# Gate sort as single-pass matmuls on 64 stacked rows, and layer 2's squares folded to one tile on VectorE

## Chip, cores, metric

One NeuronCore of a Trainium2 chip. The metric is the device time in microseconds of one execution; lower is better. TensorE is called PE in the profile, its weight loads PEld, VectorE DVE, ScalarE ACT, GpSimd POOL, and SyncE, which issues the DMAs, SP.

## What is computed

Two layers of a bidirectional hybrid encoder on 256 positions of 2048 channels in float32, and a final RMS norm. Cut to what matters here:

```
def rms_norm(x, w):
    y = xf * lax.rsqrt(jnp.mean(xf * xf, axis=-1, keepdims=True) + EPS)
    return (y * w.astype(jnp.float32)).astype(x.dtype)

def hybrid_layer(x, norm_w, w_in, b_in, ...):
    hn = rms_norm(x, norm_w)
    u = jnp.einsum("bsd,dn->bsn", hn, w_in) + b_in
    q, k, v, o, z_a, gates, glu_a, glu_b, z_b, g_a, g_b = jnp.split(u, _OFFSETS, axis=-1)
    ...
    gates = gates.astype(f32).reshape(B, S, 4, H).transpose(2, 0, 3, 1)
    i_fw, f_fw, i_bw, f_bw = gates[0], gates[1], gates[2], gates[3]
    flip = lambda t: jnp.flip(t, axis=2)
    both = lambda fw, bw: jnp.concatenate([fw, flip(bw)], axis=0)
    h2 = mlstm_chunkwise(both(qh, qh), both(kh, kh), both(vh, vh),
                         both(i_fw, i_bw), jax.nn.log_sigmoid(both(f_fw, f_bw)))
    ...
    merged = jax.nn.sigmoid(g_a) * y_a + jax.nn.sigmoid(g_b) * y_b
    return x + jnp.einsum("bsd,de->bse", merged, w_out)
```

`y_a` comes out of `h2`, `y_b` out of a gated depthwise convolution. There are 4 heads, so `gates` are 16 channels: input and forget gate, forward and backward, for each head. The backward ones are used with the positions reversed.

## The kernel before

**Data and pairs.** Activations lie with channels on the 128 partitions and the 256 positions along the free axis. Almost all of the work is products with weights of 2048 rows. The weights come in pairs of tiles (2048 rows by 256 columns), 104 pairs per layer, numbered n; each pair comes in four quarters c, which SP loads into RAW (line 324) as soon as the low part of the previous pair's quarter has been made. A float32 product is made of float32r products of high and low parts: ScalarE casts RAW to the high part (split_hi, line 438), VectorE subtracts to get the low part (split_lo, line 841), and TensorE multiplies the high part with the high and low activations at once (512 columns, line 1576) and the low part with the high activations (256 columns, line 1579). The inner step of `multiply` is two of the first kind and two of the second, 16 such instructions in a quarter. After a pair, ScalarE copies the low sums (low_half, lines 447 and 451) and VectorE adds the two (pair_out, line 848, or scaled_out, line 962, in the first pairs).

**Order.** Each engine runs its own list, written out by hand; semaphores order them. Between the splits of each pair the lists of ScalarE and VectorE hold the other work of that stage, and an engine never skips a waiting instruction. TensorE waits for `lo_made` at each quarter.

**Gates.** After the second pair of a layer TensorE multiplies the 16 gate columns, high and low part (line 1720, 128 rows by 32 columns), into one PSUM bank. ScalarE copies one half (line 568). VectorE's make_gates adds the halves (line 1016), multiplies by the norm's scale (line 1018) and adds the bias (line 1021), which sets `gates_made`. GATES are 32 rows of float32, the high columns' sums on the first 16 and the low ones' on the others. TensorE's sort_gates (lines 1731 and 1732) puts the gates in rows by head and direction, with the positions reversed for the backward half, by multiplying with the 0/1 matrix PICK: four float32 matmuls, with 32 rows and 8 columns of weights and 256 moving columns each. PICK adds rows 0 to 15 and 16 to 31 up by the way. In layer 1 sort_gates comes before the first quarter of pair 3, and turn_params (transposes of parameters, line 1640), before the third quarter of pair 2, waits for `gates_made` as well, since it writes the same PSUM. In layer 2 sort_gates comes before the last quarter of pair 2. ScalarE reads the sorted rows (lines 624, 625), makes the forget gates' logarithm (lines 627, 629), and VectorE the running sums and maxima (lines 1097 to 1116); ScalarE's Exp (line 635) closes this part. In this stretch VectorE's list also has the normalised activations (line 949) and their low parts (line 954), and ScalarE's the high parts (norm_high, line 552).

**The norm of layer 2.** While the last projection of layer 1 gives X two tiles at a time (lines 1509, 1512), ScalarE squares them (square_duo, line 468, into two of the four tiles of EW) and VectorE adds them to the two tiles of ACC (add_squares, line 940), except for the last pair of tiles. `sq_added` counts these additions. TensorE's sum_squares, before the third quarter of layer 2's first pair, sums over the channels: four float32 matmuls with a matrix of ones (line 1647), for ACC's two tiles and for EW's two with the last squares. ScalarE takes the root (line 485), VectorE the reciprocal (line 1068), and norm_group follows. Behind the squares ScalarE weighs X (line 474) and casts it (line 481) and loads the table for the root (line 822); VectorE makes the low parts (weighed_low, line 871).

**The last norm** has its own path at the end of layer 2 (lines 1526, 1533, 1655).

What sets PE's order around the sort in layer 1 and 2, and the sum:

```
if l == 0:
    multiply(n0, 2, YC, before=turn_params)
    multiply(n0, 3, Hs, h_lo, 0, late=sort_gates, at=0)
else:
    multiply(n0, 2, Hs, h_lo, l * 4, late=sort_gates)
```

Of the kernel before, what the change touches and what calls it, by code (L numbers as in the profile page):

```python
# [30 lines left out]
F32 = mybir.dt.float32  # L31
F32R = mybir.dt.float32r
ALU = mybir.AluOpType
# [4 lines left out]
L = 2  # L38
# [4 lines left out]
H = 4  # L43
HT = KT // H
# [7 lines left out]
NG = 4 * H  # L52
# [12 lines left out]
N_GLU, N_HEAD, N_GA, N_ZB, N_GB, N_OUT = KT, 10 * H, KT, KT // 2, KT, KT // 2  # L65
# [49 lines left out]
def build_trunk(nc, x, norm_w, w_in, b_in, qk_conv_w, mlstm_norm_w, w_a, dw_w, dw_b,  # L115
                ln_w, ln_b, w_b, w_out, final_norm_w, out):
    with ExitStack() as ctx:
        def sb(name, shape, dt=F32):
            return ctx.enter_context(nc.sbuf_tensor(name, shape, dt))
# [14 lines left out]
        MX = nc.alloc_sbuf_tensor_at("MX", [P, KT, S], F32R, offset=m_at)  # L134
        HEAD = sb("HEAD", [P, KT, S])
        QB = sb("QB", [P, HT, S])
        EW = sb("EW", [P, HT, S])
# [3 lines left out]
        ACC = sb("ACC", [P, 2, S])  # L141
# [4 lines left out]
        ONES = sb("ONES", [P, P])  # L146
        GBIAS = sb("GBIAS", [2 * NG, L])
        SEL = sb("SEL", [2 * NG, NG])
        PICK = sb("PICK", [2 * NG, 4, 2 * H])
        TCOL = sb("TCOL", [P, ST, 2 * H])  # L150
        ECOL = sb("ECOL", [P, 2, H, ST])
        R4 = sb("R4", [P, 2 * ST])[:]
# [17 lines left out]
        GW = M[:, 2 * HT, :].rearrange("p (k g) -> p k g", k=KT)  # L170

        GLOW, GATES = M[0:2 * NG, 2 * HT + 1, :], M[0:2 * NG, 2 * HT + 2, :]
        F_R, A_R, I_R, G_R, Z_R, N_R = (M[0:2 * H, i, :] for i in range(6))
        STACK = M[:, 2 * HT + 3, :]
        C_R = CROW[:]
# [29 lines left out]
        squared = sem("squared")  # L205
        sq_added = sem("sq_added")
        summed = sem("summed")
# [8 lines left out]
        gates_made, grows_mm = sem("gates_made"), sem("grows_mm")  # L216
# [216 lines left out]
        def _(act):  # L433
# [29 lines left out]

            def square_duo(l, d):

                act.wait_ge(sq_added, l * (N_OUT - 1) + (d + 1))
                q = d % 2
                nc.scalar.activation(EW[:, 2 * q:2 * q + 2, :], X[:, 2 * d:2 * d + 2, :], ACT.Square
                                     ).then_inc(squared, 1)
# [76 lines left out]
            for l in range(L):  # L546
# [254 lines left out]
                for d in range(N_OUT):  # L801
                    n = l * NP + AT_OUT
                    if d < N_OUT - 1 or l < L - 1:
                        split_rest(n, d, 0)
                    else:
                        nc.scalar.activation(R4[:, 2:3], EPSC[:], ACT.Sqrt)
                        act.wait_ge(sq_added, l * (N_OUT - 1) + (d + 1))
                        for t in range(2):
                            act.wait_ge(tile_out, t + 1)
                            nc.scalar.activation(EW[:, 2 + t, :], X[:, 2 * d + t, :], ACT.Square  # L810
                                                 ).then_inc(squared, 1)
                            nc.scalar.activation(HEAD[:, 2 * d + t, :], X[:, 2 * d + t, :], ACT.Identity,
                                                 scale=PAR[:, L * PARS + 2 * d + t:L * PARS + 2 * d + t + 1]
                                                 ).then_inc(xw_made, 1)
                        continue
                    act.wait_ge(pairs_out, n + (d + 3))
                    square_duo(l, d)
                    weigh_duo(l, d, (l + 1) * PARS + NORM_W + 2 * d)
                    if l < L - 1:
                        weighed_high(l + 1, d, xw_made, l * N_OUT + (d + 1))  # L820
# [13 lines left out]
        def _(dve):  # L834
            steps = Steps(dve, dve_steps)
            v = nc.vector
# [22 lines left out]
            dve.sem_inc(m_sum, 1)  # L859
            dve.wait_ge(ident_made, 1)  # L860
            steps.mark(v.tensor_tensor(SEL[:], IDENT[0:2 * NG, 0:NG], IDENT[0:2 * NG, NG:2 * NG], ALU.add))
            steps.mark(v.memset(PICK[:], 0.0))
            dve.wait_ge(nw_turned, 1)
            steps.mark(v.tensor_copy(NW[:], px[:, 3, 0:KT]))
            steps.wait()
# [2 lines left out]
            def weighed_low(at, d):  # L868

                dve.wait_ge(xw_hi, at * N_OUT + (d + 1))  # L870
                v.tensor_tensor(YC[:, 2 * d:2 * d + 2, S:2 * S], HEAD[:, 2 * d:2 * d + 2, :],
                                YC[:, 2 * d:2 * d + 2, 0:S].bitcast(F32), ALU.subtract
                                ).then_inc(xw_lo, 1)
# [21 lines left out]
                                           ALU.add))  # L895
            steps.mark(v.memset(HSEL[:, H:H + 1], 0.0))
            for group, half in enumerate((0, 0, H, H)):
                steps.mark(v.tensor_copy(PICK[:, group, half:half + H], SEL[:, group * H:(group + 1) * H]))
            steps.wait()
            dve.sem_inc(hsel_made, 1)  # L900
            dve.sem_inc(sel_made, 1)
# [34 lines left out]
            def add_squares(l, d, q):  # L936

                dve.wait_ge(squared, l * N_OUT + (d + 1))
                dve.wait_ge(sq_added, l * (N_OUT - 1) + (d + 2))
                v.tensor_tensor(ACC[:], ACC[:], EW[:, 2 * q:2 * q + 2, :], ALU.add  # L940
                                ).then_inc(sq_added, 1)

            for l in range(L):
# [69 lines left out]
                def make_gates():  # L1013

                    dve.wait_ge(gates_low, l + 1)
                    steps.mark(v.tensor_tensor(GATES, px[0:2 * NG, 0, 0:S], GLOW, ALU.add))
                    steps.wait()
                    steps.mark(v.tensor_tensor(GATES, GATES, RR[0:2 * NG, :], ALU.mult))
                    steps.wait()
                    dve.wait_ge(bias_in, 16)  # L1020
                    v.tensor_scalar(GATES, GATES, GBIAS[:, l:l + 1], None, ALU.add
                                    ).then_inc(gates_made, 1)

                def glu_unbiased(j, unit):

# [489 lines left out]
                for d in range(N_OUT):  # L1515
                    last = d == N_OUT - 1 and l == L - 1
                    if not last:
                        split_lo(n + (d + 1), 0)
                    if d > 0 and l < L - 1:
                        weighed_low(l + 1, d - 1)  # L1520
                    if not last:
                        for c in range(1, QC):
                            split_lo(n + (d + 1), c)
                    if last:
                        dve.wait_ge(sq_added, l * (N_OUT - 1) + (N_OUT + 1))
                        v.tensor_tensor(ACC[:, 0, :], ACC[:, 0, :], ACC[:, 1, :], ALU.add
                                        ).then_inc(sq_added, 1)
                        for t in range(2):
                            xt = X[:, 2 * d + t, :]
                            if t == 1:  # L1530
                                dve.wait_ge(sq_added, l * (N_OUT - 1) + (N_OUT + 2))
                                dve.wait_ge(squared, L * N_OUT)
                                v.tensor_tensor(ACC[:, 0, :], ACC[:, 0, :], EW[:, 2, :], ALU.add
                                                ).then_inc(sq_added, 1)
                            dve.wait_ge(tile_done, t + 1)
                            v.tensor_tensor(xt, xt, ps[:, 2 + t, S:2 * S], ALU.add).then_inc(tile_low, 1)
                            dve.wait_ge(tile_low, t + 1)
                            v.tensor_tensor(xt, xt, ps[:, 2 + t, 0:S], ALU.add).then_inc(tile_out, 1)
                        continue
                    add_x(2 * d, n, d)  # L1540
                    if d < N_OUT - 1:
                        add_squares(l, d, d % 2)
                if l < L - 1:
                    weighed_low(l + 1, N_OUT - 1)

            dve.wait_ge(rms_made, L + 1)
# [9 lines left out]
        def _(pe):  # L1556
            mm = nc.tensor.matmul
# [86 lines left out]
            def sum_channels(bank, tiles, done):  # L1644

                for t, tile in enumerate(tiles):
                    i = mm(px[:, bank, 0:S], ONES[:], tile, start=(t == 0),
                           stop=(t == len(tiles) - 1))
                i.then_inc(done, 1)
# [17 lines left out]
            for l in range(L):  # L1667
# [31 lines left out]

                def sum_squares():  # L1700

                    pe.wait_ge(sq_added, (l - 1) * (N_OUT - 1) + (N_OUT + 1))
                    pe.wait_ge(squared, l * N_OUT)
                    sum_channels(0, [ACC[:, t, :] for t in range(2)] + [EW[:, t, :] for t in range(2, 4)],
                                 summed)

                if l == 0:
                    turn_x(0)
# [15 lines left out]
                def sort_gates():  # L1724

                    pe.wait_ge(sel_made, 1)
                    pe.wait_ge(par_made, 1)
                    pe.wait_ge(gates_made, l + 1)
                    for kind in range(2):
                        dst = px[0:2 * H, 2, kind * S:(kind + 1) * S]  # L1730
                        mm(dst, PICK[:, kind, :], GATES, start=True, stop=False)
                        i = mm(dst, PICK[:, kind + 2, :], GATES[:, ::-1], start=False, stop=True)
                    i.then_inc(grows_mm, 1)

                if l == 0:
# [116 lines left out]
                                            HEAD[:, t, s * P:(s + 1) * P], IDENT[:])  # L1852
                return i

            pe.wait_ge(sq_added, (L - 1) * (N_OUT - 1) + (N_OUT + 3))
            column_sums(ps, [ACC[:, 0, :]], last=False)
            pe.wait_ge(xw_made, L * N_OUT - 1)
            turn_y(px, 0, 0, KT // 2).then_inc(y_turned, 1)
# [33 lines left out]
```

## Time and profile before

| | |
|---|---|
| median of 3 runs | 2401.4 us (2401.31 to 2402.68) |
| profiled execution | 2402.0 us |
| its span, first to last instruction | 2399.9 us |
| PE busy | 2388.9 us (100%), 13966 instructions |
| PEld busy | 2101.8 us (88%) |
| DVE busy | 1954.4 us (81%), 2991 instructions |
| ACT busy | 1391.6 us (58%), 1686 instructions |
| DMA | 444.61 MB, 185 GB/s, 62% of 16 engines |
| granted TensorE clock | 1.000 |

How to read it: the busy share is an average over the span. In the timelines a row gives the start in us from the span's start, the time from the start of the first to the end of the last of the instructions merged in it, engine, line of the kernel, operation, output and inputs, and x the number of instructions. An idle time of at least a tenth or so of a microsecond before it stands in brackets, with what ended it. Instructions of one engine overlap: the next may start before the last has ended. PE's ends are modelled, so the distance of starts is the better measure of what a matmul takes.

### The profile page before, as it was taken

To read this page: it belongs to the slowest core of one execution; us is meant where nothing else is said; L and a number is where in the kernel's file an instruction comes from. 1 tells how busy PE (TensorE), PEld (TensorE's weight loads), DVE (VectorE), ACT (ScalarE), POOL (GpSimd) and SP (SyncE) were. 2 spreads that over 40 slices of the span, in tenths; PEclk is the share of its full clock that TensorE was granted. 3 is DMA by queue.
4 is the path that set the end of the run, shared out by engine and by line. 5 is a ranking of instruction groups with operands and counts; after the bars stand their busy time and mean duration, and the time that the engine had idled before them with its cause. 6 is when DMAs were issued, how large, how long until landed. Compare 5 with 4: busy or idle time off the path is not lost.

```text
span 2399.9 us, 38509 instructions
## 1 busy us (share of the span) xinstructions
PE 2388.9 (100%) x13966; PEld 2101.8 (88%) x13966; DVE 1954.4 (81%) x2991; ACT 1391.6 (58%) x1686; POOL 73.0 (3%) x42
## 2 busy tenths in 40 slices
PE   9999999999999999999999999999999999999998
PEld 7888888888888888888888888888888888888887
DVE  8898989898987877556678899999999887865565
ACT  7655564646465557555565655555555655665554
POOL 0000000000000000000000000000000000000000
PEclk9999999999999999999999999999999999999999
DMA  7676656566566666665656666665656666666654
GB/s 214 190 198 192 179 176 185 178 184 178 176 193 191 187 183 199 187 192 191 181 168 192 195 184 180 181 182 175 186 174 180 190 193 192 177 200 192 190 186 140
DMA packets 448714, 444.61 MB, mean 185 GB/s; under 512 B 18032, under 2 KB 445824, under 8 KB 448640
## 3 DMA queue, kind: packets, MB, share of 16 engines
q1 hardware_dynamic: 448640, 443.74, 62.0%
q8 instruction: 32, 0.52, 0.1%
q14 instruction: 42, 0.34, 0.0%
HBM read 441.59 MB, written 2.10 MB: 185 GB/s over the span
## 4 chain that ended last, share of the span: by engine, by line
PE 93%; DVE 4%; SPq 1%; ACT 1%; DMA 1%; issue 0%; ACTq 0%; DVEq 0%
PE ps L1576 55%; PE ps L1579 28%; PE ps L1594 4%; PE ps L1598 2%; DVE W L841 1%; DVE ACC L994 1%; DMA RAW<-in_w_in_dram 1%; SPq L345 0%; PE ps L1839 0%; ACT W L438 0%; DVE HEAD L1198 0%; PE px L1773 0%; PE px L1794 0%; PE px L1772 0%; PE px L1795 0%
## 5 line engine op out<-in xcount | busy, mean ns | idle before, releaser
L1576 PE MATMUL ps<-Hs,W 128*128 128x512 f32 x4928 | 1533.3, 392 | 0.4 <-DVE W L841 0.4
L841 DVE TENSOR_TENSOR W<-RAW,W 128x1024 fp32r<-128x1024 f32 x832 | 1008.9, 1220 | 370.2 <-ACT W L438 367.5
L438 ACT CAST W<-RAW 128x1024 fp32r<-128x1024 f32 x832 | 862.3, 1049 | 699.3 <-PE ps L1579 598.2
L1579 PEld LDWEIGHTS ps<-Hs,W 128*128 128x128 f32 x4928 | 925.4, 188 | 204.5
L1579 PE MATMUL ps<-Hs,W 128*128 128x256 f32 x4928 | 972.8, 279 | 0.0
L1576 PEld LDWEIGHTS ps<-Hs,W 128*128 128x128 f32 x4928 | 747.5, 188 | 2.5 <-issue 1.5
L994 DVE SCALAR_TENSOR_TENSOR ACC<-CP,CWT,ACC 128x256 f32<-128x256 f32 x928 | 404.5, 495 | 0.2
L1576 PE MATMUL ps<-YC,W 128*128 128x512 f32 x1120 | 347.8, 392 | 0.0
L1579 PEld LDWEIGHTS ps<-YC,W 128*128 128x128 f32 x1120 | 210.3, 188 | 46.3
L1579 PE MATMUL ps<-YC,W 128*128 128x256 f32 x1120 | 221.0, 279 | 0.0
L1576 PEld LDWEIGHTS ps<-YC,W 128*128 128x128 f32 x1120 | 169.7, 188 | 0.2
L1594 PE MATMUL ps<-W,Hs 128*128 128x512 f32 x512 | 159.8, 393 | 0.0
L451 ACT ACTIVATE T<-ps,PAR 128x256 f32<-128x256 f32 x278 | 115.7, 466 | 0.0
L1598 PEld LDWEIGHTS ps<-W,Hs 128*128 128x128 f32 x512 | 96.2, 188 | 21.9
L1598 PE MATMUL ps<-W,Hs 128*128 128x256 f32 x512 | 101.1, 279 | 0.0
L1594 PEld LDWEIGHTS ps<-W,Hs 128*128 128x128 f32 x512 | 77.2, 188 | 0.0
L848 DVE TENSOR_TENSOR QB<-ps,T 128x512 f32<-128x512 f32 x107 | 73.0, 683 | 0.3 <-ACT T L447 0.3
L544 ACT ACT_TABLE_LOAD x52 | 66.7, 1283 | 0.9
L438 ACT ACT_TABLE_LOAD x50 | 64.2, 1283 | 0.9
L422 POOL TENSOR_SCALAR_AFFINE_SELECT EW<-EW 128x512 f32<-128x512 f32 x16 | 34.0, 2149 | 661.0 <-ACT EW L658 661.0
L1198 DVE SCALAR_TENSOR_TENSOR HEAD<-QPAD,PAR,HEAD 128x256 f32<-128x256 f32 x128 | 52.7, 483 | 0.0
L1198 DVE SCALAR_TENSOR_TENSOR QB<-QPAD,PAR,QB 128x256 f32<-128x256 f32 x128 | 52.0, 478 | 0.0
(234 smaller groups left out, 1183.7 us busy)
## 6 DMA issues: line engine op xcount, KB each, us to landing
RAW<-in_w_in_dram SPq DMA_DIRECT2D x640, 512.0 KB, 3.7
RAW<-in_w_a_dram SPq DMA_DIRECT2D x64, 512.0 KB, 3.4
RAW<-in_w_b_dram SPq DMA_DIRECT2D x64, 512.0 KB, 3.3
RAW<-in_w_out_dram SPq DMA_DIRECT2D x64, 512.0 KB, 4.1
M<-in_x_dram SPq DMA_DIRECT2D x4, 512.0 KB, 7.3
HEAD<-in_b_in_dram SPq DMA_DIRECT2D x8, 256.0 KB, 4.7
out_dram<-M SPq DMA_DIRECT2D x4, 256.0 KB, 3.2
out_dram<-M SPq DMA_DIRECT2D x2, 512.0 KB, 4.8
```

Of the source, the lines that this page charges most:

```text
L422: nc.gpsimd.affine_select(out=w, in_=w, compare_op=ALU.is_ge, fill=0.0, base=0, pattern=[[P * sign, ST], [-sign, S]], channel_multiplier=s ...
L438: nc.scalar.copy(WH[:, c, :, :], RAW[:, c, :, :]).then_inc(hi_made, 1)
L451: i = nc.scalar.activation(T[:, q, t, :], ps[:, 2 * q + t, S:2 * S], ACT.Identity, bias=bias(t))
L544: nc.scalar.activation(where, where, ACT.Sigmoid).then_inc(done, 1)
L841: v.tensor_tensor(WL[:, c, :, :], RAW[:, c, :, :], WH[:, c, :, :].bitcast(F32), ALU.subtract).then_inc(lo_made, 1)
L848: v.tensor_tensor(dst, ps[:, 2 * q:2 * q + 2, 0:S], T[:, q, :, :], ALU.add).then_inc(pairs_out, 1)
L994: steps.mark(v.scalar_tensor_tensor(out=dst, in0=src, scalar=w, in1=ACC[:, t, :], op0=ALU.mult, op1=ALU.add))
L1198: ins = v.scalar_tensor_tensor(out=dst[:, t, :], in0=src, scalar=w, in1=dst[:, t, :], op0=ALU.mult, op1=ALU.add)
L1576: mm(ps[:, 2 * q + t, :], WH[:, c, kk, t * P:t * P + P], act_in[:, kt, :], start=(kt == 0), stop=False)
L1579: i = mm(ps[:, 2 * q + t, S:2 * S], WL[:, c, kk, t * P:t * P + P], act_in[:, kt, 0:S], start=False, stop=(kt == KT - 1))
L1594: mm(ps[:, 2 * q + s, :].rearrange("p (a b) -> p a b", a=2), Hs[:, kt, s * P:(s + 1) * P], W[:, c, :, kk, :], start=(kt == 0), stop=False)
L1598: i = mm(ps[:, 2 * q + s, S:2 * S], Hs[:, kt, S + s * P:S + (s + 1) * P], W[:, c, 0, kk, :], start=False, stop=(kt == KT - 1))
```

## The change

GATES with the bias added is no longer kept as one float32 tile for the sort. VectorE writes it rounded to float32r on 32 rows of a new view GSPLIT (of the memory of M's tile 6), waits for that, and writes the difference of the exact and the rounded value on the next 32 rows. PICK becomes float32r and holds its 0/1 rows twice, on 64 rows, with four more small copies in the setup. The four matmuls of the sort take PICK and GSPLIT, 64 rows, float32r. For layer 2's norm VectorE now also adds the last squares to ACC and folds ACC's two tiles to one before its weighed_low of the last tiles, and TensorE's sum takes that one tile: one float32 matmul in place of four. `sq_added` counts two more steps per layer, so all waits on it have N_OUT + 1 for N_OUT - 1.

```diff
--- before.py
+++ after.py
@@ -146,7 +146,7 @@
         ONES = sb("ONES", [P, P])
         GBIAS = sb("GBIAS", [2 * NG, L])
         SEL = sb("SEL", [2 * NG, NG])
-        PICK = sb("PICK", [2 * NG, 4, 2 * H])
+        PICK = sb("PICK", [4 * NG, 4, 2 * H], F32R)
         TCOL = sb("TCOL", [P, ST, 2 * H])
         ECOL = sb("ECOL", [P, 2, H, ST])
         R4 = sb("R4", [P, 2 * ST])[:]
@@ -170,6 +170,7 @@
         GW = M[:, 2 * HT, :].rearrange("p (k g) -> p k g", k=KT)
 
         GLOW, GATES = M[0:2 * NG, 2 * HT + 1, :], M[0:2 * NG, 2 * HT + 2, :]
+        GSPLIT = MX[0:4 * NG, HT + 2, :]
         F_R, A_R, I_R, G_R, Z_R, N_R = (M[0:2 * H, i, :] for i in range(6))
         STACK = M[:, 2 * HT + 3, :]
         C_R = CROW[:]
@@ -859,7 +860,7 @@
             dve.sem_inc(m_sum, 1)
             dve.wait_ge(ident_made, 1)
             steps.mark(v.tensor_tensor(SEL[:], IDENT[0:2 * NG, 0:NG], IDENT[0:2 * NG, NG:2 * NG], ALU.add))
-            steps.mark(v.memset(PICK[:], 0.0))
+            steps.mark(v.memset(PICK[:].bitcast(F32), 0.0))
             dve.wait_ge(nw_turned, 1)
             steps.mark(v.tensor_copy(NW[:], px[:, 3, 0:KT]))
             steps.wait()
@@ -895,7 +896,9 @@
                                            ALU.add))
             steps.mark(v.memset(HSEL[:, H:H + 1], 0.0))
             for group, half in enumerate((0, 0, H, H)):
-                steps.mark(v.tensor_copy(PICK[:, group, half:half + H], SEL[:, group * H:(group + 1) * H]))
+                for rows in (slice(0, 2 * NG), slice(2 * NG, 4 * NG)):
+                    steps.mark(v.tensor_copy(PICK[rows, group, half:half + H],
+                                             SEL[:, group * H:(group + 1) * H]))
             steps.wait()
             dve.sem_inc(hsel_made, 1)
             dve.sem_inc(sel_made, 1)
@@ -936,7 +939,7 @@
             def add_squares(l, d, q):
 
                 dve.wait_ge(squared, l * N_OUT + (d + 1))
-                dve.wait_ge(sq_added, l * (N_OUT - 1) + (d + 2))
+                dve.wait_ge(sq_added, l * (N_OUT + 1) + (d + 2))
                 v.tensor_tensor(ACC[:], ACC[:], EW[:, 2 * q:2 * q + 2, :], ALU.add
                                 ).then_inc(sq_added, 1)
 
@@ -1018,8 +1021,12 @@
                     steps.mark(v.tensor_tensor(GATES, GATES, RR[0:2 * NG, :], ALU.mult))
                     steps.wait()
                     dve.wait_ge(bias_in, 16)
-                    v.tensor_scalar(GATES, GATES, GBIAS[:, l:l + 1], None, ALU.add
-                                    ).then_inc(gates_made, 1)
+                    high = GSPLIT[0:2 * NG, :]
+                    steps.mark(v.tensor_scalar(high, GATES, GBIAS[:, l:l + 1], None, ALU.add))
+                    steps.wait()
+                    v.scalar_tensor_tensor(out=GSPLIT[2 * NG:4 * NG, :], in0=GATES,
+                                           scalar=GBIAS[:, l:l + 1], in1=high.bitcast(F32),
+                                           op0=ALU.add, op1=ALU.subtract).then_inc(gates_made, 1)
 
                 def glu_unbiased(j, unit):
 
@@ -1541,6 +1548,10 @@
                     if d < N_OUT - 1:
                         add_squares(l, d, d % 2)
                 if l < L - 1:
+                    add_squares(l, N_OUT - 1, (N_OUT - 1) % 2)
+                    dve.wait_ge(sq_added, l * (N_OUT + 1) + (N_OUT + 2))
+                    v.tensor_tensor(ACC[:, 0, :], ACC[:, 0, :], ACC[:, 1, :], ALU.add
+                                    ).then_inc(sq_added, 1)
                     weighed_low(l + 1, N_OUT - 1)
 
             dve.wait_ge(rms_made, L + 1)
@@ -1699,10 +1710,8 @@
 
                 def sum_squares():
 
-                    pe.wait_ge(sq_added, (l - 1) * (N_OUT - 1) + (N_OUT + 1))
-                    pe.wait_ge(squared, l * N_OUT)
-                    sum_channels(0, [ACC[:, t, :] for t in range(2)] + [EW[:, t, :] for t in range(2, 4)],
-                                 summed)
+                    pe.wait_ge(sq_added, l * (N_OUT + 1) + 2)
+                    sum_channels(0, [ACC[:, 0, :]], summed)
 
                 if l == 0:
                     turn_x(0)
@@ -1728,8 +1737,8 @@
                     pe.wait_ge(gates_made, l + 1)
                     for kind in range(2):
                         dst = px[0:2 * H, 2, kind * S:(kind + 1) * S]
-                        mm(dst, PICK[:, kind, :], GATES, start=True, stop=False)
-                        i = mm(dst, PICK[:, kind + 2, :], GATES[:, ::-1], start=False, stop=True)
+                        mm(dst, PICK[:, kind, :], GSPLIT, start=True, stop=False)
+                        i = mm(dst, PICK[:, kind + 2, :], GSPLIT[:, ::-1], start=False, stop=True)
                     i.then_inc(grows_mm, 1)
 
                 if l == 0:
```

Left out are four hunks that only change N_OUT - 1 to N_OUT + 1 in waits on `sq_added` (lines 466, 807, 1525, 1530, 1855).

## Rows read from the trace of the kernel before

**Rows 1.** The page: busy time and share of TensorE, and the chain that ended last.

```profile
PE 2388.9 (100%) x13966; PEld 2101.8 (88%) x13966; DVE 1954.4 (81%) x2991; ACT 1391.6 (58%) x1686; POOL 73.0 (3%) x42
...
PE 93%; DVE 4%; SPq 1%; ACT 1%; DMA 1%; issue 0%; ACTq 0%; DVEq 0%
```

**Rows 2.** Timeline of TensorE at the layer 2 sort: start us, length us, engine, line.

```profile
1236.46 0.39 PE L1579 MATMUL ps<-Hs,W 128*128 128x256 f32 x2
1236.79 0.59 PE L1731 MATMUL px<-M,PICK 32*8 32x256 f32 x2
...
1238.08 0.59 PE L1732 MATMUL px<-M,PICK 32*8 32x256 f32 x2
...
1239.18 0.40 PE L1579 MATMUL ps<-Hs,W 128*128 128x256 f32 x2
```

**Rows 3.** Timeline of TensorE around layer 2's sum of squares.

```profile
1206.12 0.40 PE L1579 MATMUL ps<-YC,W 128*128 128x256 f32 x2
...
1208.55 0.40 PE L1579 MATMUL ps<-YC,W 128*128 128x256 f32 x2
...
1209.24 0.39 PE L1579 MATMUL ps<-YC,W 128*128 128x256 f32 x2
```

**Rows 4.** Timeline of TensorE at the gate projection of layer 2.

```profile
1224.70 3.85 PE L1720 MATMUL px<-YC,GS 128*32 128x512 f32 x16
1228.39 0.63 PE L1576 MATMUL ps<-Hs,W 128*128 128x512 f32 x2
```

**Rows 5.** Timeline of ScalarE at the start of layer 2.

```profile
1204.76 0.63 ACT L468 ACTIVATE EW<-X 128x512 f32<-128x512 f32 x1 [2.61 <-DVE X L1512]
...
1206.86 1.28 ACT L822 ACT_TABLE_LOAD   x1
...
1209.19 0.47 ACT L485 ACTIVATE RR<-px,EPSC 128x256 f32<-128x256 f32 x1
```

**Rows 6.** Timelines of VectorE, and last of TensorE, at the start of layer 2.

```profile
1206.87 0.69 DVE L871 TENSOR_TENSOR YC<-HEAD,YC 128x512 fp32r<-128x512 f32 x1 [2.15 <-ACT YC L481]
...
1210.46 1.75 DVE L1068 RECIPROCAL RR<-RR 128x256 f32<-128x256 f32 x1
...
1220.54 1.22 DVE L841 TENSOR_TENSOR W<-RAW,W 128x1024 fp32r<-128x1024 f32 x1
...
1221.89 0.65 PE L1576 MATMUL ps<-YC,W 128*128 128x512 f32 x2
```

**Rows 7.** Timelines of ScalarE and VectorE around the gates of layer 2.

```profile
1232.39 0.91 ACT L575 ACTIVATE QB<-QB,PAR 128x256 f32<-128x256 f32 x2 [3.78 <-DVE QB L965]
...
1236.30 0.34 DVE L1021 TENSOR_SCALAR M<-M,GBIAS 32x256 f32<-32x256 f32 x1
...
1244.50 1.05 ACT L438 CAST W<-RAW 128x1024 fp32r<-128x1024 f32 x1 [0.97 <-PE ps L1579]
```

**Rows 8.** Timelines of the three engines in the first pairs of layer 1.

```profile
43.95 0.34 DVE L1021 TENSOR_SCALAR M<-M,GBIAS 32x256 f32<-32x256 f32 x1
44.22 1.20 DVE L949 TENSOR_TENSOR HEAD<-HEAD,RR 128x1024 f32<-128x1024 f32 x1
...
52.28 1.04 ACT L552 CAST Hs<-HEAD 128x1024 fp32r<-128x1024 f32 x1 [1.35 <-DVE HEAD L949]
...
75.54 1.23 DVE L841 TENSOR_TENSOR W<-RAW,W 128x1024 fp32r<-128x1024 f32 x1 [2.52 <-ACT W L438]
...
76.90 0.73 PE L1576 MATMUL ps<-Hs,W 128*128 128x512 f32 x2 [0.40 <-DVE W L841]
```

**Rows 9.** Durations by line (ns min/median/max), and VectorE's timeline in the setup.

```profile
L1162 DVE SCALAR_TENSOR_TENSOR GS<-CROW,MASK,GS x4: 468/472/475, 205.8 to 1392.9; 8x256 fp32r<-8x256 f32 x4
...
L1526 DVE TENSOR_TENSOR ACC<-ACC x1: 424/424/424, 2382.6 to 2382.6; 128x256 f32<-128x256 f32 x1
...
L940 DVE TENSOR_TENSOR ACC<-ACC,EW x14: 692/693/694, 1128.1 to 2381.8; 128x512 f32<-128x512 f32 x14
...
6.95 0.88 DVE L886 TENSOR_SCALAR HEAD<-px,NW 128x256 f32<-128x256 f32 x2 [2.73 <-PE px L1628]
```

More of the change, by code:

```diff
@@ L464, in square_duo @@
             def square_duo(l, d):
-                act.wait_ge(sq_added, l * (N_OUT - 1) + (d + 1))
+                act.wait_ge(sq_added, l * (N_OUT + 1) + (d + 1))
                 q = d % 2
@@ L806, in _ @@
                         nc.scalar.activation(R4[:, 2:3], EPSC[:], ACT.Sqrt)
-                        act.wait_ge(sq_added, l * (N_OUT - 1) + (d + 1))
+                        act.wait_ge(sq_added, l * (N_OUT + 1) + (d + 1))
                         for t in range(2):
@@ L1524, in _ @@
                     if last:
-                        dve.wait_ge(sq_added, l * (N_OUT - 1) + (N_OUT + 1))
+                        dve.wait_ge(sq_added, l * (N_OUT + 1) + (N_OUT + 1))
                         v.tensor_tensor(ACC[:, 0, :], ACC[:, 0, :], ACC[:, 1, :], ALU.add
@@ L1530, in _ @@
                             if t == 1:
-                                dve.wait_ge(sq_added, l * (N_OUT - 1) + (N_OUT + 2))
+                                dve.wait_ge(sq_added, l * (N_OUT + 1) + (N_OUT + 2))
                                 dve.wait_ge(squared, L * N_OUT)
@@ L1543, in _ @@
                 if l < L - 1:
+                    add_squares(l, N_OUT - 1, (N_OUT - 1) % 2)
+                    dve.wait_ge(sq_added, l * (N_OUT + 1) + (N_OUT + 2))
+                    v.tensor_tensor(ACC[:, 0, :], ACC[:, 0, :], ACC[:, 1, :], ALU.add
+                                    ).then_inc(sq_added, 1)
                     weighed_low(l + 1, N_OUT - 1)
@@ L1853, in turn_y @@
                 return i
-            pe.wait_ge(sq_added, (L - 1) * (N_OUT - 1) + (N_OUT + 3))
+            pe.wait_ge(sq_added, (L - 1) * (N_OUT + 1) + (N_OUT + 3))
             column_sums(ps, [ACC[:, 0, :]], last=False)
```

## The prediction

> **What bounds the kernel now.** I read the page first: TensorE is busy for the whole span, and the chain that ended last lies on it for 93% [rows 1]. At first sight every TensorE microsecond that goes comes off the end. The remaining shares of that chain warn against it: 4% VectorE and 1% ScalarE have to be somewhere. So the second view is the timeline of TensorE at the two places that the change touches [rows 2, 3], and the third the timelines of the other two engines around them [rows 5 to 8], to see what TensorE waits for next once it arrives earlier. "Arrives" is always at the next quarter of a weight pair, whose low part VectorE must have made (line 841).
>
> **What the sort takes.** In layer 2 the reader sees L1579 at 1236.46, the four sort matmuls from 1236.79, and the first later L1579 at 1239.18: 2.72 us [rows 2]. Without the sort it would be 0.69, the distance of the L1579 pairs at 1208.55 and 1209.24 [rows 3]. So the sort costs 2.03. From 1236.79 to 1238.08 three matmuls pass, 0.43 each, each recorded as two instructions (x2 in the row): four take 1.72. The other 0.31 is 0.10 on entering and 0.21 on leaving this small form. In layer 1 the same pattern stands once more, from 51.65 to 54.37, with the same 2.72.
>
> A float32r matmul of 512 columns takes 0.23 (16 gate matmuls before L1576 at 1228.39, 3.69 us) [rows 4]. A period of 0.69 holds two of those and two of 256 columns, so one of 256 takes 0.115. I price the four new ones at that, 0.46 together, as stacking on 64 rows adds no columns. The loads of PICK's eight columns lie beside them. From above the bound is 0.43 each (no gain, as before), from below 0.115, which I take, as it is the same type and number of columns.
>
> The 0.31 for the change of form: the gate matmuls, 128 rows by 32 columns, show none on leaving, L1576 following at the 0.23 beat [rows 4]; the sort, 32 by 8, shows 0.31. The new form is 64 by 8. I keep 0.31, the nearer row by columns; 0 is the other end. New sort: 0.77, so 1.26 less TensorE time per layer.
>
> The Trainium skill, TensorEngine Tiling (Array Packing), Key Properties, says that changing the tiling mode drains the engine, and lists a 64-row mode beside the 32-row one. By that rule the 0.31 stays, and the trace agrees for 32 rows; were there no such drain, the total below would be 0.31 us lower.
>
> **What the sum of squares takes.** From L1579 at 1206.12 to L1579 at 1208.55 is 2.43, less 0.69: four float32 matmuls cost 1.74, or 0.435 each [rows 3]. Three go: 1.30 less TensorE time, once.
>
> **What VectorE gets.** For the sum: the last pair of squares is ready when L468 ends, 1204.76 + 0.63 = 1205.39 [rows 5]. The new addition takes 0.69 and the fold 0.42 [rows 9], to about 1206.55 with the wait between them. VectorE is idle for 2.15 us up to 1206.87, when it takes L871 [rows 6], so both fit and nothing behind them moves. If that cover were gone, they would cost 1.1. TensorE, naturally at this point at 1206.35 (1206.12 and two of 0.115), waits some 0.3 for the fold; only then does its one matmul run.
>
> For the gates: L1021 keeps its place and about its 0.34, and writes the high part; then comes a wait for it, and a SCALAR_TENSOR_TENSOR of 256 columns. Nearest row: L1162, same operation with a pointer scalar and an fp32r output, 0.472 [rows 9]. The other forms, 0.41 and 0.50, bound it. In layer 1, L1021 ends at 44.29 and the next instruction had started at 44.22, 0.07 before the end [rows 8]; with the extra one it starts at 44.29 + 0.47 - 0.07, plus some hundredths for the wait: **0.5 us later**. The gates are ready 0.5 later too, in both layers, and TensorE waits for them (turn_params in layer 1, sort_gates in layer 2).
>
> Setup: four more copies into PICK, a tenth of a microsecond each, lie in VectorE's 2.73 us of idleness before L886 [rows 9]: nothing. No DMA is added or moved, and neither SP's queue nor POOL's is passed by anything.
>
> **Layer 1: the saving is lost, the addition is not.** At 76.90 TensorE starts a pair after waiting for L841 of 75.54 [rows 8]. Followed back, that comes from ScalarE's weight cast, its table loads (line 635's Exp and the return to the cast), the sigmoid of L544, VectorE's L848, three L841 and the gate rows (L1097 to L1116), ScalarE's Ln and Exp of L627 and L629, and so to L552 at 52.28, which waited for VectorE's L949 [rows 8]. VectorE works without a gap from before line 1021 up to that L949 (no row between the two has an idle time), so what is added at 1021 reaches it in full. No step of this chain waits for the sort: ScalarE comes to read its result (L624) only after the sigmoid of L575, three casts and L447, which all stand behind L552 in its list. So TensorE, 0.5 late into the sort and 1.26 shorter in it, stands still longer before VectorE's low parts, at 76.90 at the latest, and starts when VectorE lets it: 0.5 later than now. **Layer 1: +0.5.** From 77 on TensorE is the bound, and everything up to layer 2 keeps that shift.
>
> **Layer 2, sum of squares: nothing.** ScalarE goes from L468 through the table load of 1206.86 to L485 at 1209.19 without a gap; with the sum ready at 1207.2 instead of 1208.2, L485 still starts at 1209.19 [rows 5]. VectorE's reciprocal follows at 1210.46, and it then runs without a gap to L841 at 1220.54, which ends at 1221.76. TensorE starts the quarter that needs it at 1221.89 [rows 6]: 0.13 of slack, which is about what a start after a wait takes anyway. So the 1.0 us net that TensorE has gained by then (1.30 less the 0.3) is stood off here. I take 0, between -0.1 and +0.1; even these don't reach the sort, which waits for VectorE.
>
> **Layer 2, sort: this one counts.** The gates are ready at 1236.30 + 0.34 = 1236.64, and the sort starts at 1236.79 [rows 2, 7]; the two arrive together now. That time of VectorE hangs on ScalarE's sigmoid at 1232.39 [rows 7] and through VectorE's gapless run on 1210.46, so it doesn't move with TensorE. The sort starts 0.5 later and is 1.26 shorter: -0.76. What is late next: the chain of gate rows behind it starts with ScalarE's L438 at 1244.50, which waited for TensorE (0.97, L1579) [rows 7], so it moves along with TensorE. **Layer 2: -0.76.**
>
> **Sum:** +0.5 + 0 - 0.76 = -0.26. The profiled execution took 2402.0 (span 2399.9, 2.1 around it): 2401.7 for it. The median of the three runs, 2401.4, is 0.6 lower, so I forecast a median of **2401.2**, no change that a measurement can tell (0.2% of it is 4.8 us).
>
> **Rivals.**
> (a) TensorE is the bound everywhere [rows 1], and all that it loses counts: 1.30 + 2 x 1.26 = 3.8 less, 2397.6. For it: the shares. Against: the waits and gapless runs above. It holds in part if VectorE's chain in layer 1 has a link that I read as tight and that isn't: then layer 1 gives -0.76 too and the total is -1.5, 2399.9. Chance 0.08 for the whole, 0.08 for the part.
> (b) Slower: the sort's single-pass matmuls are no quicker, because with eight columns or a reversed input they are paced by something other than passes. Then layer 2 keeps only the later gates: +0.5 + 0.5 = +1.0, 2402.4. It decides once the four take over 1.2 us together (0.3 each); below this the sum stays negative. For it: no row has a reversed float32r operand. Against: reversed and straight float32 ones take the same 0.43 [rows 2]. The same number comes out if the change doesn't do what it says, the compiled matmuls keeping two instructions each. Chance 0.08.
> (c) The fold comes so late that TensorE's sum, and with it ScalarE's root (L485), moves. The sum must be there by 1209.19 and is expected at 1207.2, so the first 2.0 us of lateness are free; an addition queued behind L871 instead of before it would be done at 1206.87 + 0.69 + 1.1 = 1208.7, still (just) in time. Only TensorE waits more: with its one matmul done at about 1209.2 instead of four at 1208.1, it comes 1.1 late to the sort where the gates are 0.5 late, so the sum rises by 0.6 to +0.3, 2402.3. Chance 0.03.
>
> **Numbers.** The forecast has 0.73. The range: the case without the 0.31 (-0.57), the partial (a) at 2399.9 and (b) at 2402.4, widened by the spread of runs (2401.3 to 2402.7 for the same kernel): 2399.6 to 2403.0. Full (a) is left out. Faster by over 0.2% would take 4.8 us, more than the whole 3.8 of (a): 0.01. Slower by as much has no mechanism priced near it: 0.01.
>
> **What would show it.** Sort matmuls as one record each, 0.115 apart, with gaps of 0.1 and 0.2 around them. TensorE's start at 76.90 moved to 77.4, with stalls between the sort and it longer by 1.26 in all, and by 0.5 before turn_params. A pause of 0.3 before the single sum matmul, and the quarter at 1221.89 starting after a wait of about 1 us; L485 and the reciprocal at the same distance from L468 as before. The layer 2 sort starting 0.12 after VectorE's new instruction. I am wrong if the 76.90 start comes earlier than now, if the reciprocal moves towards L468, or if the span drops by over 2 us.

## The result and the profile after

The changed kernel is 0.2% slower: median 2406.95 us of 14 runs (2404.80 to 2407.77) against 2401.64 for the kernel before (14 runs, 2400.39 to 2402.68), ratio 1.0021 with a 95% interval of 1.0014 to 1.0029. The forecast was 2401.2 with a range up to 2403.0. The profiled execution took 2405.61, its span is 2403.9.

First the page of the changed kernel: the span, the busy times, the chain, and of part 5 the matmuls and the casts.

```profile
span 2403.9 us, 38489 instructions
...
PE 2387.4 (99%) x13952; PEld 2101.5 (87%) x13952; DVE 1957.3 (81%) x2999; ACT 1392.5 (58%) x1686; POOL 75.9 (3%) x42
...
PE 91%; DVE 4%; issue 2%; ACT 1%; SPq 1%; DMA 1%; DVEq 0%; ACTq 0%
...
L1587 PE MATMUL ps<-Hs,W 128*128 128x512 f32 x4928 | 1534.7, 393 | 5.1 <-DVE W L842 5.1
```

TensorE is busy 1.5 us less than in [rows 1], with 14 fewer instructions, and the span is 4.0 longer. The chain has 2% "issue", where it had 0%: time in which an engine waited for nothing that the profile shows. TensorE's large matmuls waited 5.1 us for VectorE's low parts (0.4 before, for the same group). TensorE's busy time did fall, as the change meant it to; the time was lost elsewhere.

**Where.** Laid side by side by TensorE's large matmuls, the two traces lie within about 0.5 us of each other up to 1263, except just behind layer 1's sort and layer 2's sum, where the changed kernel is up to 1.3 ahead and loses it in the next wait. Then comes this, VectorE of the changed kernel at the jump back of layer 2's loop over the convolution (columns: start us, length us):

```profile
1324.24 0.69 DVE L1006 TENSOR_TENSOR CP<-QB 128x512 f32 x1 [0.84 <-ACT QB L545]
1330.99 0.18 DVE L979 COPY CWT<-PAR 128x31 f32 x1 [6.05 <-issue]
...
1331.53 1.23 DVE L842 TENSOR_TENSOR W<-RAW,W 128x1024 fp32r<-128x1024 f32 x1
```

The same place in the kernel before:

```profile
1324.90 0.69 DVE L1003 TENSOR_TENSOR CP<-QB 128x512 f32 x1 [0.84 <-ACT QB L544]
1325.76 0.19 DVE L976 COPY CWT<-PAR 128x31 f32 x1 [0.17 <-DVE CP L1003]
...
1327.12 1.23 DVE L841 TENSOR_TENSOR W<-RAW,W 128x1024 fp32r<-128x1024 f32 x1 [0.81 <-ACT W L438]
```

Between the last instruction of the loop's first round and the first of its second VectorE stands still for 6.05 us, waiting for no semaphore. The DMA view of this stretch (1320 to 1332) has a row of a queue that carries instructions, which the kernel before doesn't have there (columns: queue and kind, packets, MB, share of 16 engines):

```profile
q14 instruction: 4, 0.03, 1.1%
```

TensorE needs the low part that is late, and then does this:

```profile
1328.76 0.62 PE L1587 MATMUL ps<-Hs,W 128*128 128x512 f32 x2
...
1332.88 0.73 PE L1587 MATMUL ps<-Hs,W 128*128 128x512 f32 x2 [3.26 <-DVE W L842]
1333.45 0.40 PE L1590 MATMUL ps<-Hs,W 128*128 128x256 f32 x2
1333.69 1.01 PE L1587 MATMUL ps<-Hs,W 128*128 128x512 f32 x2
1334.50 0.63 PE L1590 MATMUL ps<-Hs,W 128*128 128x256 f32 x2
1334.93 1.05 PE L1587 MATMUL ps<-Hs,W 128*128 128x512 f32 x2
...
1336.21 1.05 PE L1587 MATMUL ps<-Hs,W 128*128 128x512 f32 x2
...
1337.33 0.63 PE L1587 MATMUL ps<-Hs,W 128*128 128x512 f32 x2
```

A period is two matmuls of each of the two lines; [rows 3] has it at 0.69 between L1579 pairs. Three periods, from 1333.69 to 1337.33, take 3.64 us, where three of 0.69 would be 2.07: 1.57 lost. The windows of the changed kernel show the granted clock beside it (columns: window, its length, busy us of each engine with their instructions, clock, DMA share, GB/s):

```profile
1329.00:1333.00 4.00, 0.74 (x5) 0.49 (x4) 2.01 (x7) 1.78 (x3) 0.00 (x0) 1.00 0.01 4
1333.00:1337.10 4.10, 4.10 (x15) 3.43 (x16) 4.10 (x10) 0.00 (x0) 0.00 (x0) 0.59 0.58 148
1337.10:1345.00 7.90, 7.90 (x48) 6.97 (x47) 7.90 (x13) 3.17 (x3) 0.00 (x0) 1.00 0.85 249
```

After TensorE had stood for 3.26 us its mean granted clock over 4.1 us was 0.59: the lower level (1.2 of 2.4 GHz) for most of them. Then it was at full again. The starts before and after the wait (1328.76 and 1333.69) are 4.93 apart, 3.55 more than two periods. 3.55 + 1.57 = 5.1, which is the distance that the traces gain on each other between 1263 and 1385. Of the difference of the spans, 4.0, the rest is small and negative: 0.5 before 1263, and 0.6 behind 1385, 0.4 of it near 1845, where TensorE of the kernel before waits (0.24 by the profile) and this one doesn't.

### The profile page after: what moved, and what is told of

It reads as the page before. It is cut to its first block, busy times and chain, and to the rows that moved or that the text cites. A ratio compares the mean times of both kernels' runs of the same rounds, so it can differ in the third digit from the quotient of the medians.

```text
span 2403.9 us, 38489 instructions
## 1 busy us (share of the span) xinstructions
PE 2387.4 (99%) x13952; PEld 2101.5 (87%) x13952; DVE 1957.3 (81%) x2999; ACT 1392.5 (58%) x1686; POOL 75.9 (3%) x42
## 4 chain that ended last, share of the span: by engine, by line
PE 91%; DVE 4%; issue 2%; ACT 1%; SPq 1%; DMA 1%; DVEq 0%; ACTq 0%
PE ps L1587 54%; PE ps L1590 27%; PE ps L1605 5%; PE ps L1609 2%; DVE W L842 1%; DVE ACC L997 1%; DMA RAW<-in_w_in_dram 1%; ACT W L439 0%; SPq L346 0%; DVE HEAD L952 0%; PE px L1782 0%; PE px L1803 0%; PE px L1781 0%; PE px L1783 0%; PE px L1804 0%
## 5 line engine op out<-in xcount | busy, mean ns | idle before, releaser
L1590 PEld LDWEIGHTS ps<-Hs,W 128*128 128x128 f32 x4928 | 926.2, 188 | 204.8
L1590 PE MATMUL ps<-Hs,W 128*128 128x256 f32 x4928 | 973.2, 279 | 0.0
L1590 PEld LDWEIGHTS ps<-YC,W 128*128 128x128 f32 x1120 | 210.3, 188 | 46.3
L1590 PE MATMUL ps<-YC,W 128*128 128x256 f32 x1120 | 221.0, 279 | 0.0
```

The lines of the kernel that those rows point to most:

```text
L1590: i = mm(ps[:, 2 * q + t, S:2 * S], WL[:, c, kk, t * P:t * P + P], act_in[:, kt, 0:S], start=False, stop=(kt == KT - 1))
```

## The experiments

Theory A, which the runs below are to decide: VectorE fetches its instructions in blocks, and a loop that doesn't lie within two of them has to fetch its head again at the jump back. The change adds 9 instructions to VectorE's list ahead of layer 2's loop: the setup's four copies, a SCALAR_TENSOR_TENSOR each for the gates of layers 1 and 2, and three for the sum of squares (two additions and a wait); the first six belong to the sort, the last three to the squares. In the program's list for VectorE, counted from 0, the loop of 260 instructions moves from 1705-1964 to 1714-1973. Rivals: the new instructions themselves delay layer 2 (B for the gates, C for the squares), or their mere number does (D).

**One half of the change each.** First the sort alone: the changed kernel, with the squares as they were.

```diff
-                    add_squares(l, N_OUT - 1, (N_OUT - 1) % 2)
...
-                    sum_channels(0, [ACC[:, 0, :]], summed)
+                    sum_channels(0, [ACC[:, t, :] for t in range(2)] + [EW[:, t, :] for t in range(2, 4)],
+                                 summed)
```

Then the squares alone: the changed kernel, with the gates, `PICK` and the sort as they were.

```diff
-                        mm(dst, PICK[:, kind, :], GSPLIT, start=True, stop=False)
+                        mm(dst, PICK[:, kind, :], GATES, start=True, stop=False)
...
```

> The gate sort alone (64 stacked rows, float32r), the sum of squares as before. Theory A, code position: VectorE's list is 6 instructions longer up to layer 2's convolution loop; the loop of 260 instructions then still begins and ends within two blocks of 256 instructions, so no pause at its jump back; 0.3 us less than before (layer 1 +0.5, layer 2 -0.76), 2401.3. Theory B, the new dependent pair of VectorE instructions is what delays layer 2 (the conversion or the later gates pile up until the convolution): the pause of VectorE of about 6 us near 1325 is there, and the time is that of the changed kernel, 5 us over before.

> The sum of squares alone (VectorE adds and folds, TensorE one matmul in place of four), the sort as before. Theory A: VectorE's list is 3 instructions longer up to layer 2's loop, no pause there; TensorE gains 1.0 us at the sum and loses it before the quarter near 1221.9 in a wait for line 841, so within 0.1 us of before, 2401.6. Theory C, the additions on VectorE or the wait that TensorE gets at the sum cost the 5 us: the time is about 2406.

Measured: the sort alone 2400.89 us, ratio 0.9998 (0.9989 to 1.0007); the squares alone 2401.05, ratio 0.9999 (0.9990 to 1.0008); the kernel before in this group 2401.28. Neither has a pause near 1325. Each half is harmless and the two together cost 5 us, so neither B nor C, the work itself, is the cause.

**Instructions that do nothing.** Here the kernel before gets 8 memsets ahead of all loops, the changed one 2 (the diff shows the 8):

```diff
+        PADS = sb("PADS", [P, 8])
...
             v.memset(EPSC[:], EPS)
+            for i in range(8):
+                v.memset(PADS[:, i:i + 1], 0.0)
```

> The kernel before, with 8 memsets of one column each to an unused tile at the head of VectorE's list, where VectorE waits anyway. Nothing else changes. Theory A: the loop of layer 2 now ends on the first instruction of a third block, so its jump back is followed by a pause of VectorE of some 6 us near 1325, TensorE waits over 3 us for line 841, its granted clock falls to half for some us after it, and the time is 4.5 to 5.5 us over before, 2406 to 2407. Theories B and C: nothing of the change is in it, so the time is that of before, within 0.1 us.

> The changed kernel with 2 such memsets in front. Theory A: the loop of layer 2 now begins on the first instruction of a block and lies in two; no pause, and the time falls by about 5 us to 2401.3, 0.3 under before. Theories B and C: the changed kernel's time stays, about 2406.9.

Measured: 2406.20, ratio 1.0020 (1.0011 to 1.0029), for the kernel before with 8 memsets; 2400.88, ratio 0.9999 (0.9990 to 1.0008), for the changed one with 2. VectorE of the former at the jump:

```profile
1329.39 0.19 DVE L979 COPY CWT<-PAR 128x31 f32 x1 [4.20 <-issue]
1331.71 0.15 DVE L981 COPY CWT<-PAR 128x1 f32 x1 [2.14 <-issue]
```

and TensorE behind it:

```profile
1333.47 0.73 PE L1579 MATMUL ps<-Hs,W 128*128 128x512 f32 x2 [3.60 <-DVE W L842]
...
1335.18 1.05 PE L1579 MATMUL ps<-Hs,W 128*128 128x512 f32 x2
```

Nearly the whole loss (4.9 us over the kernel before in this group, 2401.28) comes back with nothing of the change in the kernel, with the slow matmuls behind it; in the changed kernel it goes with two memsets more.

**The same memsets behind the loops.** The 8 lines stand ahead of VectorE's wait for the last `rms_made` (`L + 1`) in place of the head.

> Control of the third run: the kernel before with the same 8 memsets, but near the end of VectorE's list, behind both layers' loops and before the last reciprocal, where VectorE waits for ScalarE. Theory A (where the loop lies among the blocks of 256 instructions): layer 2's loop lies where it lay before, no pause near 1325, the time is within 0.3 us of before (0.1 to 0.3 if the memsets delay the last reciprocal). Theory D, the number of VectorE's instructions or the extra tile costs it: 2406.

Measured: 2400.54, ratio 0.9998 (0.9989 to 1.0007), before in this group 2401.07. No pause near 1325. D falls, and with it the extra tile as a cause.

**The edge.** 7 memsets on the kernel before, 1 on the changed one.

> The third run with 7 memsets in place of 8. Theory A in its sharp form (the pause comes only when the loop reaches a third block): the loop ends on the last instruction of its second block, no pause near 1325, 2401.1. In a softer form, which the runs so far suggest for the loop of 285 instructions (a pause of 2.8 us with its last instruction second or first before the block's end): one fetch, a pause of some 3 us, of which TensorE sees 1 to 2 us or nothing: 2401.1 to 2403.

> The changed kernel with 1 memset in front in place of 2. Theory A: the loop's first instruction is now the last of a block, and the loop still reaches into a third: the pause stays, in two parts of which the first ends after one register instruction and not two, and the time stays 4.5 to 5.5 us over before, 2405.6 to 2406.8, though the kernel with one memset more has 2400.9.

Measured: 2401.01, ratio 0.9999 (0.9990 to 1.0008), and 2406.38, ratio 1.0021 (1.0012 to 1.0030). The kernel before in this group had 2401.16. VectorE at the jump, first with 7 memsets on the kernel before, then with 1 on the changed one:

```profile
1324.89 0.69 DVE L1006 TENSOR_TENSOR CP<-QB 128x512 f32 x1 [0.84 <-ACT QB L545]
1325.75 0.19 DVE L979 COPY CWT<-PAR 128x31 f32 x1 [0.17 <-DVE CP L1006]
```

```profile
1324.75 0.69 DVE L1009 TENSOR_TENSOR CP<-QB 128x512 f32 x1 [1.19 <-ACT QB L546]
1331.85 0.18 DVE L982 COPY CWT<-PAR 128x31 f32 x1 [6.41 <-issue]
```

Together the eight placements of this loop read:

```
kernel                      loop in VectorE's list   pause at the jump     median us
before                      1705 to 1964             none                  2401.3
squares alone               1708 to 1967             none                  2401.05
sort alone                  1711 to 1970             none                  2400.89
before, 7 memsets           1712 to 1971             none                  2401.01
before, 8 memsets           1713 to 1972             4.20 + 2.14           2406.20
changed                     1714 to 1973             6.05 in all           2406.95
changed, 1 memset           1715 to 1974             6.41 in all           2406.38
changed, 2 memsets          1716 to 1975             none                  2400.88
```

From 1320 to 1332 the instruction queue has packets with 8 memsets and with 1 memset too (3 each), and none in the sort alone and with 7.

The second part of the pause tells where a block begins. The trace's records of register instructions, which the timelines leave out, show it where no work does: with 8 memsets three instructions of the loop pass before it (two register ones and the first copy), in the changed kernel two, with 1 memset one. In all three that ends at 1716. And the pause appears when the loop's last instruction goes from 1971 to 1972, 256 after 1716. With 1 memset L1009, the loop's last but two, is the instruction at 1972, and it waits 1.19 where the others have 0.84: 0.35 more for going on into a new block, against some 6 for the jump back. So blocks begin at 1716 and 1972. This loop jumps back freely from the blocks on both sides of 1716; when it has reached a third it pays twice: once for its head, once for the block behind it, which begins one to three instructions later.

The Trainium skill, Runtime: NRT & Kernel Launch, Instruction fetch mechanics, says that most engines hold two blocks of 256 instructions, filled in order, and that a taken branch to a target outside of them waits for a DMA fetch. The trace agrees with the 256 and with the two, and the row of the instruction queue above shows the fetch itself; its price here is 4.2 and 2.1 us for the two fetches.

**The same pause where the low parts are ahead.**

> The changed kernel with 8 memsets in front. Theory A: layer 2's convolution loop lies in two blocks, no pause near 1325; but layer 1's loop of 285 instructions beside the sigmoid gates (first at 702) now spans three blocks, so VectorE pauses some 5 to 6 us at its jump back near 765. There the low parts are 5.8 us ahead of TensorE, against 1.6 to 1.8 at the jump near 1325, so TensorE waits at most 1 us: 2401 to 2402.2. Against it, a theory by which any pause of this size costs the same whatever the lead: 2406.

Measured: 2400.73, ratio 0.9998 (0.9989 to 1.0007). The loop of 285 instructions lies at 1180 to 1464 of the list. VectorE at its jump:

```profile
763.64 0.69 DVE L1374 TENSOR_TENSOR M<-QB 128x512 f32 x1
766.06 0.19 DVE L982 COPY CWT<-PAR 128x31 f32 x1 [1.73 <-issue]
```

There is a pause, but of 1.73 and not of the 5 to 6 that were expected. The DMA view from 755 to 775 has the same four packets of the instruction queue, so again more than the head comes; but here 22 instructions of the head's block are left to run, and the second fetch doesn't show (this reason is argued, not tested). TensorE waits for nothing between 700 and 800. That a pause costs only what exceeds the lead of the low parts is in keeping with this, and with the 2.75 us that the changed kernel with 2 memsets has at this jump at no cost; a pause of 6 us where the low parts are 5.8 ahead is not among the runs.

The edge of this loop is as sharp as that of the other. The program's list counts jumps that merely lead from one part to the next and that VectorE doesn't run: from the head of this loop to that of the loop near 1325 it has 542 instructions in the changed kernel, while the trace holds 540 records when each loop is counted once. So in this loop's numbers the block beginnings two and one before 1716 are not 1204 and 1460 but 2 less, 1202 and 1458. The runs put this loop's last instruction on both sides of it:

```
kernel                      loop in VectorE's list   pause near 765, us   instruction packets, 755 to 775
changed                     1172 to 1456             none                 none
changed, 1 memset           1173 to 1457             none                 none
changed, 2 memsets          1174 to 1458             2.75                 4
before, 7 memsets           1174 to 1458             2.87                 4
before, 8 memsets           1175 to 1459             2.82                 4
changed, 8 memsets          1180 to 1464             1.73                 4
```

This loop pauses exactly where it has reached a third block, in the two kernels with transposes below as well, and TensorE waits for nothing there. Two loops of different length thus have their edges two blocks of 256 apart.

**TensorE's time in the two layers.** The step of the prediction about who sets the time, on the changed kernel with 2 memsets, which has no pause near 1325, with 12 transposes more behind one of the two sorts (`l == 0` in the first kernel, `l > 0` in the second):

```diff
                     i.then_inc(grows_mm, 1)
+                    if l == 0:
+                        keep_clock(3, 12)
```

> On the changed kernel with 2 memsets in front, 12 more transposes on TensorE behind layer 1's sort (about 1.4 us of TensorE). The step of the prediction: TensorE is not the bound there, VectorE's chain sets its starts near 68 and 77, so the waits before them shrink by 1.4 us and the time stays within 0.2 us of 2400.9. The rival, TensorE the bound everywhere: 1.4 us more, 2402.3.

> The same 12 transposes behind layer 2's sort. The step of the prediction: here TensorE's time counts in full, as ScalarE's and VectorE's next work waits for it: 1.3 to 1.4 us more than the changed kernel with 2 memsets, 2402.2 to 2402.4. If the sort's saving in layer 2 had been lost as well, the 12 transposes would cost under 0.5 us.

Measured: 2400.40 with them in layer 1 and 2401.88 in layer 2, on the same chip beside each other: 1.48 apart, where the twelve take 1.28 (52.55 to 53.83 below). Each one's interval of 0.1% against the kernel before (2401.07) is wider than that, but the runs themselves hardly overlap (2400.13 to 2401.49, and 2401.31 to 2402.85), and the traces decide. TensorE in layer 1 with them, and its two waits:

```profile
52.55 1.53 PE L1623 MATMUL px<-IDENT 128*128 128x128 f32 x12
53.83 0.70 PE L1590 MATMUL ps<-Hs,W 128*128 128x512 f32 x2
...
68.07 0.74 PE L1590 MATMUL ps<-Hs,W 128*128 128x512 f32 x2 [0.17 <-DVE W L843]
...
77.03 0.73 PE L1590 MATMUL ps<-Hs,W 128*128 128x512 f32 x2 [0.40 <-DVE W L843]
```

Without them (the layer 2 kernel, same stretch):

```profile
68.27 0.73 PE L1590 MATMUL ps<-Hs,W 128*128 128x512 f32 x2 [1.42 <-DVE W L843]
...
77.22 0.72 PE L1590 MATMUL ps<-Hs,W 128*128 128x512 f32 x2 [0.38 <-DVE W L843]
```

The wait near 68 falls by 1.25 and the start behind it moves by no more than 0.2. Side by side, the kernel with the twelve in layer 2 drops back against the other by 1.33 at layer 2's sort (1238), and 2.23 behind there is still 2.15 behind at the end. Layer 1 has over a microsecond of TensorE time to give away, layer 2's sort has none.

## Why the prediction was wrong

**The steps that were costed held.** The timelines of the changed kernel, TensorE and VectorE at layer 2's sort and sum:

```profile
1236.68 0.39 PE L1590 MATMUL ps<-Hs,W 128*128 128x256 f32 x2
1237.53 0.27 PE L1740 MATMUL px<-MX,PICK 64*8 64x256 f32 x1 [0.47 <-DVE MX L1027]
1237.65 0.28 PE L1741 MATMUL px<-MX,PICK 64*8 64x256 f32 x1
...
1238.67 0.40 PE L1590 MATMUL ps<-Hs,W 128*128 128x256 f32 x2
```

```profile
1206.35 0.40 PE L1590 MATMUL ps<-YC,W 128*128 128x256 f32 x2
1206.85 0.70 PE L1658 MATMUL px<-ACC,ONES 128*128 128x256 f32 x2
...
1207.86 0.40 PE L1590 MATMUL ps<-YC,W 128*128 128x256 f32 x2
...
1222.04 0.73 PE L1587 MATMUL ps<-YC,W 128*128 128x512 f32 x2 [0.66 <-DVE W L842]
```

```profile
1205.64 0.69 DVE L943 TENSOR_TENSOR ACC<-ACC,EW 128x512 f32<-128x512 f32 x1 [0.70 <-ACT EW L469]
1206.37 0.43 DVE L1553 TENSOR_TENSOR ACC<-ACC 128x256 f32<-128x256 f32 x1
1207.10 0.69 DVE L872 TENSOR_TENSOR YC<-HEAD,YC 128x512 fp32r<-128x512 f32 x1 [0.30 <-ACT YC L482]
```

- The sort: one record for each matmul, 0.12 apart. From its first matmul to the L1590 behind it 1.14, against 2.39 in [rows 2]: 1.25 shorter (1.26 forecast). In layer 1 it takes 0.77, as forecast. The change of form to 64 rows costs what it cost at 32.
- The sum: 1.51 from L1590 to L1590, less 0.69, is 0.82 where it was 1.74: 0.92 less (1.0 forecast). The two additions fit in VectorE's idle time, of which 0.30 is left, against the 2.15 in [rows 6]. The gain is gone at 1222.04, in the wait of 0.66 that was foreseen.
- The gates: VectorE's way from line 1021 (1018 before) to the instruction behind the gates is 1.33, against 0.72: **0.61** and not 0.5, as the next one starts 0.50 behind the start of the SCALAR_TENSOR_TENSOR and not 0.40. From there to TensorE's start near 76.9 it is 34.04, against 33.40: this reaches the start in full, as said. The start itself lies at 76.94 and not at 77.4, because in this execution VectorE came to the gates 0.60 earlier (42.46 for 43.06): a start alone doesn't show the 0.6, the distance does.
- Layer 2: from ScalarE's square (L469, 1204.98; 1204.76 in [rows 5]) to the L1590 behind the sort 33.69, against 34.42: -0.73 (-0.76 forecast).

The changed kernel freed of the pause is 0.4 under the kernel before beside it (2400.88 to 2401.28), which the intervals of 0.1% can't tell from the -0.26 of the sum nor from nothing. Two figures of the rivals are off, and nothing hangs on them. In (b) the sum turns positive once the four matmuls take over 1.72 less the 1.0 of the two delays, 0.72 us; 1.2 is where layer 2 alone does. In (c) +0.3 on the median of 2401.4 gives 2401.7, not 2402.3.

**The step that failed** is one that wasn't taken. The change part by part counted instructions by their time and by the waits they cause; the term for where they push the code was missing. The term was put at nothing without being named: "nothing" for the setup's four copies, and "fit and nothing behind them moves" for the additions, are true of their time and false of their place: with the two SCALAR_TENSOR_TENSORs and a wait they are the nine that bring the loop's end from 1964 past 1971. "It moves along with TensorE" holds up to the jump near 1325, where the chain that starts with L438 gets 6 us of VectorE's own. And "slower by as much has no mechanism priced near it" read the absence of any such pause in the trace before as its absence from the machine: no row of before shows it, since all its loops happened to jump freely, this one with 7 instructions to spare. In place of the forecast -0.26 the medians are 5.3 apart, and in the profiled executions this one jump loses 5.1.

Why 6 us of pause are 3.55 of wait is the lead again: the low part behind the jump is ready only 1.6 us before TensorE wants it in the kernel before (it ends at 1328.35, the quarter starts at 1329.97), and VectorE had another 1 us of waits there that the pause swallowed (0.17 and 0.81). Of the 5.1 us, 3.55 are the wait and 1.57 the matmuls at the lower clock.

## What to carry to other kernels

An edit that adds or takes a few instructions on an engine with loops can move the time by microseconds that belong to none of them. Look for a pause marked "issue" at a jump back and for packets of the instruction queue beside it, and try the kernel with a few empty instructions in front before judging the edit. Of VectorE's loops here, those longer than one block of 256 instructions paused exactly where they had reached into a third block: for the 260 instructions that is when the head sits in the last three places of a block, for the 285 in the last 28, of which three were tried. The loop of 28 instructions never paused. A shift cured it; a shorter body should as well, which no run tried. What such a pause costs depends on how far its product is ahead of the engine that is the bound: at one loop the fetch was free, at the other 6 us cost 5.

## What the runs showed of the hardware

- A fetch at a jump: 4.20 and 2.14 us of VectorE's idle time for two in a row, 1.73 for one whose follower was hidden. The two halves of a change can each be free and cost 5 us together.
- Both edges lie exactly where a loop's last instruction becomes the first of a third block: 1971 and 1972 for the loop near 1325, 1457 and 1458 for the one near 765, which are two blocks apart once the jumps that VectorE doesn't run are left out of the count. Going on into a new block cost 0.35 at the one place where a timeline shows it (L1009, 1.19 for 0.84). Why the loop near 765 pauses 2.8 us when it ends on the first or second place of the third block and 1.73 when on the seventh stays open.
- TensorE's granted clock was 0.59 in the mean over 4.1 us behind a standstill of 3.3 us, and 1.00 from 69 to 72 behind the standstill of 1.4 near 68 in layer 1.
